# Five waits ahead of the experts, and the order of gate, up and down in a hybrid layer with 32 experts

## The reference

```python
u = rmsnorm(h); proj = u @ w_in                     # q, k, v, xb, gb, z, xbc, dt
o_a = stick_breaking(q, k, v)                       # attention, 8 heads x 64
o_b = rglru_branch(xb, gb); o_c = ssd_branch(z, xbc, softplus(dt + dt_bias))
gates = sigmoid(u @ w_gate + b_gate)                # three gates of 1024
merged = sum(gates[b] * (o[b] @ w_branch_out[b]) for b in range(3))
h = h + merged @ w_out
u = rmsnorm(h)                                      # router: best of 4 groups, then best 2 of its 8 experts
for e in range(32):                                 # rows routed to e, scattered back with their weight
    h[rows] += weight * ((silu(x[rows] @ w_gate_e) * (x[rows] @ w_up_e)) @ w_down_e)
return rmsnorm(h)
```

## Time and profile before

| | us |
|---|---|
| runs shown, median | 1225.12 (1225.67, 1225.12, 1219.31) |
| profiled execution | 1222.56 |
| its span, first to last instruction | 1220.8 |
| PE busy / DVE / ACT / POOL in the span | 1121.6 / 529.3 / 385.5 / 184.6 |
| mean granted clock of PE, share of full speed | 0.977 |
| moved by DMA | 263.11 MB |

### The profile page before, as it was taken

How to read it: one execution, slowest core, us unless ns; L and a number is a source line. 1 busy time by engine, 2 the same in 40 slices (tenths; PEclk the granted TensorE clock), 3 DMA queues, 4 the chain that set the end, 5 groups by cost and what they waited for, 6 DMA issues and landing times.

```text
span 1220.8 us, 17206 instructions
## 1 busy us (share of the span) xinstructions
PE 1121.6 (92%) x6833; PEld 795.5 (65%) x6833; DVE 529.3 (43%) x992; ACT 385.5 (32%) x602; POOL 184.6 (15%) x196
## 2 busy tenths in 40 slices
PE   4999799999999999999999879999999999999994
PEld 4898677777988899999999853433333333333342
DVE  4341567663246465543534642333333333333335
ACT  4313666666547444433431101111111111111113
POOL 6000011211213346542310010000000000000000
PEclk9999899999999999999999959999999999999997
DMA  9268443452222212225362299999999999999972
GB/s 184 81 127 111 35 53 44 52 52 37 56 65 63 77 53 70 61 81 153 87 222 98 83 376 404 426 426 428 428 428 427 427 426 429 428 426 428 406 282 79
DMA packets 94312, 263.11 MB, mean 216 GB/s; under 512 B 5020, under 2 KB 75896, under 8 KB 81960
## 3 DMA queue, kind: packets, MB, share of 16 engines
q1 hardware_dynamic: 87664, 250.36, 59.1%
q0 software_dynamic: 3456, 6.58, 1.5%
q10 hardware_dynamic: 3128, 5.29, 1.2%
HBM read 258.24 MB, written 7.64 MB: 218 GB/s over the span
## 4 chain that ended last, share of the span: by engine, by line
PE 57%; DMA 26%; DVE 7%; ACT 5%; issue 3%; SPq 1%; POOL 0%; DVEq 0%; ACTq 0%; POOLq 0%
DMA arena<-in_w_expert_up 22%; PE za L1129 12%; PE pj L765 10%; PE pj L766 10%; PE pj L767 10%; PE pj L792 2%; PE zb L1149 2%; DMA arena<-in_x_prompt 2%; DMA ring<-in_w_in 1%; DVE arena L1748 1%; DVE arena L1747 1%; PE zb L900 1%; ACT arena L1355 1%; DVE arena L1780 1%; ACT arena L1357 1%
## 5 line engine op out<-in xcount | busy, mean ns | idle before, releaser
L1129 PE MATMUL za<-arena 128*64 128x512 f32 x1024 | 229.8, 603 | 26.2 <-DMA arena<-in_w_expert_up 25.3
L765 PE MATMUL pj<-u_high_r,ring_r 128*128 128x288 f32 x736 | 224.0, 304 | 1.2 <-ACT arena L1279 1.1
L767 PE MATMUL pj<-u_high_r,ring_r 128*128 128x288 f32 x736 | 216.7, 294 | 0.0
L766 PE MATMUL pj<-u_rest_r,ring_r 128*128 128x288 f32 x736 | 216.7, 294 | 0.0
L1129 PEld LDWEIGHTS za<-arena 128*64 128x64 f32 x1024 | 72.3, 139 | 175.5 <-issue 138.1
L765 PEld LDWEIGHTS pj<-u_high_r,ring_r 128*128 128x128 f32 x736 | 138.1, 188 | 14.1 <-issue 10.2
L766 PEld LDWEIGHTS pj<-u_rest_r,ring_r 128*128 128x128 f32 x736 | 138.2, 188 | 0.6
L767 PEld LDWEIGHTS pj<-u_high_r,ring_r 128*128 128x128 f32 x736 | 138.0, 188 | 0.0
L1630 DVE TENSOR_TENSOR ring_r<-ring,ring_r 128x1024 fp32r<-128x1024 f32 x62 | 78.4, 1270 | 105.5 <-ACT ring_r L1246 105.4
L1149 PE MATMUL zb<-arena 128*64 128x512 f32 x512 | 113.4, 595 | 4.3 <-DVE arena L2104 2.7
L1149 PEld LDWEIGHTS zb<-arena 128*64 128x64 f32 x512 | 36.2, 137 | 74.6 <-issue 73.3
(11 more groups left out here) (428 smaller groups left out, 2083.2 us busy)
## 6 DMA issues: line engine op xcount, KB each, us to landing
arena<-in_w_expert_gate SPq DMA_DIRECT2D x32, 2048.0 KB, 16.2
arena<-in_w_expert_up SPq DMA_DIRECT2D x32, 2048.0 KB
arena<-in_w_expert_down SPq DMA_DIRECT2D x32, 2048.0 KB
ring<-in_w_in SPq DMA_DIRECT2D x26, 512.0 KB, 9.0
ring<-in_w_gate SPq DMA_DIRECT2D x24, 512.0 KB, 4.2
arena<-in_x_prompt SPq DMA_DIRECT2D x8, 512.0 KB, 8.5
ring<-in_w_branch_out SPq DMA_DIRECT2D x8, 512.0 KB, 3.4
ring<-in_w_in SPq DMA_DIRECT2D x2, 1024.0 KB, 14.8
```

The source lines that it names most:

```text
L765: pe.matmul(out, left[0], right[0], start=k == 0, stop=False)
L766: pe.matmul(out, left[0], right[1], start=False, stop=False)
L767: return pe.matmul(out, left[1], right[0], start=False, stop=k == last - 1)
L1129: m = pe.matmul(za[j * BLK:(j + 1) * BLK, b, :], xT[:, k, j * BLK:(j + 1) * BLK], w[:, j * KD + k, :], start=k == 0, stop=k == KD - 1)
```

## The change

- **Root table.** ACT takes a root of zeros as its first instruction, before it has x.
- **Split order.** ACT and DVE split the first tile of u and the first v weights before they turn to the second tile.
- **Small loads.** The rows of constants and the dt weights are issued by POOL behind its masks, when the second half of the v weights has landed; the router weights at the head of lru_weights.
- **Dt softplus.** The job dt_turn is taken off ACT's and DVE's lists. Its parts run inside att_scores: the first DVE part at unit 2, Exp at unit 3, one DVE operation and Ln at unit 4, the eleven others at unit 6.
- **First output item.** It waits for one piece of merged at a time, and the second item for all.
- **Experts.** PE's order per pair becomes up, transposes of the next pair's rows, scatters 0 to 5, gate of the next pair, transposes of the hidden rows, scatters 6 to 9, down. The rows and the gate tile have two buffers. SP's order follows: up i, gate i + 1, down i. In the last pair the first five scatters stand inside down's second half, with banks of their own, and are added there. The overflow count is read behind pair 1. The loop covers pairs 2 to 13.

```diff
@@ buffers
+        xT, gate_t = [xT, at(u2_off, KD, P)], [gate_t, at(u2_off + D, DE)]
...
+        def last_bank(k):
+
+            return (pj, za, zb)[k % NT // 2][:, k % NT % 2, :]
...
@@ SP
             load("up", None, 0, EPAIRS)
+            load("gate", None, 1, 1 + EPAIRS, 1)
+
+            sp.wait_ge(S["xg_in"], 16)
             load("down", None, 0, EPAIRS)
-
-            sp.wait_ge(S["xg_in"], 16)
-            load("gate", None, 1, 1 + EPAIRS, 1)
-            with sp.Fori(0, EPAIRS // 2 - 1) as ii:
+            load("gate", 2, 2, 2 + EPAIRS, 0)
+            load("up", 1, 1, 1 + EPAIRS)
+            load("down", 1, 1, 1 + EPAIRS)
+            with sp.Fori(1, EPAIRS // 2 - 1) as ii:
                 for turn in range(2):
                     i = 2 * ii + turn
-                    load("gate", i + 2, i + 2, i + 2 + EPAIRS, turn)
-                    load("up", i + 1, i + 1, i + 1 + EPAIRS)
-                    load("down", i + 1, i + 1, i + 1 + EPAIRS)
+                    load("up", i, i, i + EPAIRS)
+                    load("gate", i + 1, i + 1, i + 1 + EPAIRS, 1 - turn)
+                    load("down", i, i, i + EPAIRS)
             last = EPAIRS - 1
+            load("up", last - 1, last - 1, last - 1 + EPAIRS)
+            load("gate", last, last, last + EPAIRS, 1)
+            load("down", last - 1, last - 1, last - 1 + EPAIRS)
             load("up", last, last, last + EPAIRS)
             load("down", last, last, last + EPAIRS)
...
@@ PE: first output item
-                    if n == OUT0:
+                    if n == OUT0 + 1:
                         pe.wait_ge(S["mix_rest"], NMIX + 2 * KD)
                     for k in range(KD):
+                        if n == OUT0:
+                            pe.wait_ge(S["mix_rest"], NMIX + 2 * k + 1)
...
@@ PE: a pair of experts
+            def expert_pair(i, spare, ahead=None, behind=2, over=None, last=False):
+                pe.wait_ge(S["wu_in"], (i + 1) * 32)
+                into(i, 1, w_u, spare, "up_done")
+                if ahead is not None:
+                    if behind > 0:
+                        pe.wait_ge(S["hidt_r"], i)
+                    turn_rows(i + 1, 1 - spare)
+                if behind > 0:
+                    scatter(i - 1, range(6), behind > 1)
+                if ahead is not None:
+                    pe.wait_ge(S["gate_mul"], i + 1)
+                    gate(i + 1, ahead, 1 - spare)
                 pe.wait_ge(S["hid_r"], i + 1)
...
-                    scatter(i - 1, (8, 9))
+                if behind > 0:
+                    scatter(i - 1, range(6, 2 * NT))
                     pe.wait_ge(S["sc_r"], 2 * NT * (i - 1) + 8)
                 pe.wait_ge(S["hidt_r"], i + 1)
                 pe.wait_ge(S["wd_in"], (i + 1) * 32)
...
+                down(i, 0, range(DE // P))
+                if last:
+                    down(i, 1, range(DE // P // 2))
+                    scatter_last(range(NT))
+                    down(i, 1, range(DE // P // 2, DE // P))
+                else:
+                    down(i, 1, range(DE // P))
...
@@ PE (ACT and DVE alike): the count of overflow slots is read ahead of the loop
+            pe.wait_ge(S["routed"], 2)
+            turn_rows(0, 0)
+            gate(0, (0, 0), 0)
+            expert_pair(0, 0, ahead=(1, 0), behind=0)
+            expert_pair(1, 1, ahead=(0, 1), behind=1)
             pe.wait_ge(S["routed"], 3)
             total = pe.value_load(over_total[0:1, 0:1], min_val=0, max_val=OVB)
+            with pe.Fori(1, EPAIRS // 2 - 1) as ii:
...
@@ ACT: dt in the attention units (DT_RAW, DT_EXP, DT_LOG, DT_END = 2, 3, 4, 6)
                 act.activation(b, b, ACT.Exp).then_inc(S["ln_e"], 1)
+                if u == DT_EXP:
+                    dt_exp()
                 act.wait_ge(S["ln_e"], u + 1)
                 act.activation(b, b, ACT.Ln, bias=1.0).then_inc(S["l_r"], 1)
+                if u == DT_LOG:
+                    dt_log()
...
@@ ACT: a pair of experts
+            def gate(i, spare):
                 act.wait_ge(S["xt2_ps"], i + 1)
...
                 act.wait_ge(S["gate_done"], i + 1)
-                act.activation(gate_t, za[:, 0, :], ACT.Tanh, scale=0.5).then_inc(S["gate_th"], 1)
+                act.activation(gate_t[spare], za[:, 0, :], ACT.Tanh, scale=0.5).then_inc(S["gate_th"], 1)
+
+            def expert_pair(i, spare, ahead=True, before=True, over=None):
+                if ahead:
+                    gate(i + 1, 1 - spare)
                 act.wait_ge(S["hidt_ps"], i + 1)
                 act.activation(hidT, oa[:, :].rearrange("p (k l) -> p k l", k=4), ACT.Copy).then_inc(S["hidt_r"], 1)
...
@@ ACT: start
+            act.wait_ge(S["pool_c"], 1)
+            act.activation(rstd[:, NT:NT + 1], att_s[:, 0, 0:1], ACT.Sqrt)
             x_norm(0)
             x_norm(1)
             gain_up()
             u_split(0)
+            v_split(0)
+            v_split(1)
             u_split(1)
-            for j in range(4):
-                v_split(j)
+            v_split(2)
+            v_split(3)
             x_norm(2)
...
@@ DVE: dt behind the scores of units 2, 4 and 6 (dt_turn cut into dt_raw, dt_one, dt_end)
                                          ).then_inc(S["nab_r"], 1)
+                if u == DT_RAW:
+                    dt_raw()
+                if u == DT_LOG:
+                    dt_one()
+                if u == DT_END:
+                    dt_end()
...
@@ DVE: a pair of experts
+                if ahead:
+                    rows_in(i + 1, 1 - spare)
+                if behind > 0:
+                    add(i - 1, range(6), behind > 1)
+                if ahead:
+                    gate(i + 1, 1 - spare)
+                if behind > 0:
+                    add(i - 1, range(6, 10), behind > 1)
...
+                        if last and q == 0:
+                            add_last(range(NT))
...
@@ DVE: start
             x_turn(0)
+            u_split(0)
+            v_split(0)
             x_turn(1)
-            u_split(0)
+            v_split(1)
             u_split(1)
-            for j in range(4):
-                v_split(j)
+            v_split(2)
+            v_split(3)
...
@@ POOL: small loads
-            for lo, n, name in ((0, 8, "ssm_dt_bias"), (8, 8, "ssm_a_log"), (16, 8, "ssm_d"),
-                                (24, 4, "b_router_group"), (28, 32, "b_router_expert")):
-                pool.dma_start(rowc[:, lo:lo + n], a[name][0:1, :].partition_broadcast(P)
-                              ).then_inc(S["bc_in"], 16)
-            pool.dma_start(w_dt, a["w_in"][0, :, 4096:4104].rearrange("(k p) n -> p k n", p=P)
-                           ).then_inc(S["par_in"], 16)
...
+            pool.wait_ge(unit_in[3], 16)
+            pool.dma_start(w_dt, a["w_in"][0, :, 4096:4104].rearrange("(k p) n -> p k n", p=P)
+                           ).then_inc(S["par_in"], 16)
+            for lo, n, name in ((0, 8, "ssm_dt_bias"), (8, 8, "ssm_a_log"), (16, 8, "ssm_d"),
+                                (24, 4, "b_router_group"), (28, 32, "b_router_expert")):
+                pool.dma_start(rowc[:, lo:lo + n], a[name][0:1, :].partition_broadcast(P)
+                              ).then_inc(S["bc_in"], 16)
...
             def lru_weights():
+                for lo, k, name in ((0, NG, "w_router_group"), (NG, NE, "w_router_expert")):
+                    pool.dma_start(w_r[:, :, lo:lo + k], a[name][0].rearrange("(k p) n -> p k n", p=P)
+                                   ).then_inc(S["side_dma"], 16)
```

More of the change, by code:

```diff
@@ L84 @@
 ROUND = 12582912.0
+DT_RAW, DT_EXP, DT_LOG, DT_END = 2, 3, 4, 6
 TOK0 = 1024
@@ L1102, in scatter_over, with turn_rows @@
                 pe.wait_ge(S["over_r"], 2 * NT * (j + 1))
-            def expert_pair(i, turn, before=True, over=None, first=False):
-                mix = before and over is None
+            def turn_rows(i, spare):
                 pe.wait_ge(S["xg_in"], (i + 1) * 16)
-                if before:
-                    pe.wait_ge(S["hidt_r"], i)
-                else:
-                    pe.wait_ge(S["routed"], 2)
                 for k in range(KD):
@@ L1116, in expert_pair, with into, gate @@
                 m.then_inc(S["xt2_ps"], 1)
-                if mix:
-                    scatter(i - 1, range(6), not first)
+            def into(i, b, w, spare, done):
+                for k in range(KD):
+                    for j in range(2):
+                        m = pe.matmul(za[j * BLK:(j + 1) * BLK, b, :], xT[spare][:, k, j * BLK:(j + 1) * BLK],
+                                      w[:, j * KD + k, :], start=k == 0, stop=k == KD - 1)
+                m.then_inc(S[done], 1)
+            def gate(i, turn, spare):
+                par, n_turn = turn
@@ L1132, in expert_pair, with down @@
-                if mix:
-                    scatter(i - 1, (6, 7))
+                pe.wait_ge(wg_in[par], (n_turn + 1) * 32)
+                into(i, 0, w_g[par], spare, "gate_done")
+            def down(i, q, ks):
+                for k in ks:
```

(25 more changed lines are left out.)

124 lines of the change are left out of this document (65 added, 59 removed).

## The result

| | before | changed | 
|---|---|---|
| median of 17 runs, us | 1225.08 | 1217.81 |
| span from the lowest to the highest | 1219.16 to 1227.22 | 1214.18 to 1219.79 |
| ratio, with its 95% interval | | 0.9945 (0.9934 to 0.9957) |
| profiled execution, its span | 1222.56, 1220.8 | 1217.82, 1216.0 |
| mean granted clock of PE | 0.977 | 0.969 |

The change gains 7.3 us, 0.55%; 1212 was forecast, within 1203 to 1219. The sum behind the forecast, 11.7 us, was too large, and its largest term is the one that failed. PE does the same instructions in both kernels, but is busy 4.7 us longer in the changed one, 4.0 of them ahead of the issue of up 0, at a lower mean clock: where that lies on the chain of work it is a cost that the prediction had no term for.

The account below looks back on a forecast made before the run. PE bounds the kernel before the experts, weight loads at 427 GB/s bound the experts. -6.4 - 2.7 - 2.2 - 0.4 = -11.7 takes 1222.56 to 1210.9; half the median's 2.6 excess gives 1212, range 1203 to 1219 (8 in 10).

Parts of the forecast that it names:

- largest term: Kernel start: third item starts at 22.2 without the hole, at full clock, and ends at 25.1 instead of 31.69; -6.4.
- my sum: Whole kernel: the case that the summed terms hold, 1206 to 1217 us; chance 0.62.
- the front is absorbed: Rival, chance 0.15: v weights' second half late for its own size, unit 6 stalls fully; -2.5 -1.5 -2.2 = -6, 1218.
- The start: First three items: earlier root, new split order and moved small loads let the third item end earlier; -6.4.
- The reason for the late data is in the same view: Start, 11 to 15 us: small per-partition pieces fill the engines at 68 GB/s; without them the second half lands at 16 to 17.
- The prediction's own sign of being wrong: Start: ACT still waiting for w_in past 20 us would show the forecast wrong.
- The lower bound: Start: if the data doesn't come earlier, only -2.5 is left.
- Dt: Attention: second unit's scores start 5.35 earlier without the job, paid back +0.6 in units 3 and 4, +2.05 at unit 6; -2.7.
- The first output item: Before the first output item: PE starts when half 0 is done instead of waiting 2.5 for the last chunk; -2.2.
- The experts: Experts to the end: two holes in the weight flow go, one comes, the tail shrinks by 2.8; -0.4, bounds -5 to +6.
- The hole at down 1: Start of the experts: down 1 is issued at 759.4, after the gate and down 0, leaving the flow empty; +3.9.
- the tail: End, behind the last down: 22.2 us falls by 2.8 to 19.4, the overflow read moving forward.

Follow-up runs that it names:

- the second run: The kernel before with only the early root table and the new split order: ratio 1.0026 (1.0007 to 1.0045).
- the last run on the kernel before: The kernel before with unread products filling PE's waits, 28 of them at unit 0's values: ratio 0.9967 (0.9953 to 0.9981), median 1220.45 against 1224.88.

## Why the prediction was right, and where it was wrong

The range held, in part by luck. 1217.81 lies outside "my sum" (1206 to 1217) and at the number of the rival "the front is absorbed", 1218, which had 0.15; but the rival's terms (-2.5, -1.5, -2.2 and nothing from the experts) were not what the traces show either.

**The start** was the wrong step: -6.4 forecast (its own ends, 25.1 for 31.69, make 6.6), 0.0 measured. Root table and order did what was said (root 1.0 earlier, first item at 14.68 for 15.0). "The reason for the late data is in the same view" failed: the view of busy engines and bytes does not say whose packets fill them, and the view by queue did. The prediction's own sign of being wrong came, ACT waiting for the weights past 20 us (23.98), and up 0 was issued 2.1 us earlier and not 11. The lower bound was wrong too ("only -2.5 is left" if the data doesn't come earlier): as the second run shows, with the third item bound to the data nothing is left. The third item then ran at the low clock in both kernels, 1.7 and 1.4 us, where the forecast had the full one.

**Dt** was right in its parts, except that the long wait is that of unit 0's values and not of unit 1: 134.49 for 139.85 is -5.4, the payback +0.4 at unit 3 (0.6 taken) and 1.80 at unit 6 (2.05 taken). The stretch gave 4.5 instead of 2.7, since the low stretch that stood behind the long wait in before (1.7) went with the wait.

**The first output item**: -2.3 for -2.2.

**The experts**: -2.7 by the trace for -0.4, the mechanism as told; the experts' part alone brought 2.1 by the trace and no gain that the time shows. The hole at down 1 measured 4.1 for 3.9. The last up's product starts at 1174.81; by my sum 1177.7 less the 1.9 that the front was ahead, 1175.8. From there to the end of down it took 22.5 for 23.3, and the tail 18.7 for 19.4. Three small terms, each 0.7 to 1.0 too large. That the hole's removal would be worth 3.9, as its price suggested, was not so (0.9).

**The clock** had no term in the sum but at the third item. The two profiles lost 4.9 and 9.5 us before the experts, of which 3.4 and 6.5 lie on the chain. Each low stretch takes 1.7 us of PE's work or a multiple, less where PE also waits in it, and in these traces comes at a wait of PE of 1.1 us or more, but not every such wait brings one: behind the same wait at unit 16 there was one in the changed kernel's profile and none in before's, and in the run with gate 1 moved, whose instructions before the experts are the same, a longer one and another at unit 3. That the loss is the changed kernel's own is ruled out by the last run on the kernel before, where filling gained 4.4 us. What decides at a single wait is open.

Without the low stretches on the chain the profiles are 4.8 + 3.1 = 7.9 us apart: 2.8 for dt, 2.3 at the first output item, 2.7 in the experts and 0.4 in the rest, less 0.3 at the start. So the size of 11.7 came near by two errors that cancel in part: the start's too large, the experts' too small. The profiles show 4.8 of the 7.9, the medians of the runs 7.3: before's median lies 2.5 us above its profiled execution, the changed kernel's on it.

## What to carry to other kernels

When the DMA engines are full and move little, ask the trace by queue whose packets they are and how long one takes, before a load is blamed. A larger piece for the same bytes brought the weights 5.7 us sooner here, though the packets' time was not set by their size alone; try it, and look at an earlier window before the size is called the cause. A wait that is shortened ahead of one for data gives nothing; follow the chain to the next arrival. Waits of PE of one to seven microseconds cost more than their length where the clock falls at them and the chain goes on through PE; unread products that fill them are cheap, if they stand exactly where PE waits. At the start of a trace check the clock column against the pace of like products.

## What was not expected of the hardware

- A piece of 1 KB and one of 2 KB from the same weights took 194 ns each of an engine's time in 11 to 15 us, but 72 and 158 ns in 6 to 8 us.
- Low stretches of PE's clock come at some short waits and not at others, and what decides is open: behind 1.56 us at the same instruction the clock was 1.00 in one profile and 0.50 in another, 1.7 us of work each time or a multiple of it. In the spread of the runs, 8 us for before, several such steps fit: of the 77 runs of before beside the experiments the 21 under 1222 us had a mean granted clock of 0.976, the other 56 of 0.971.
